# Down-projections with two slices of the second panel first, norm rows by a repeated column, a last norm on three engines, and a new order of some copies and low parts

## What is computed

```python
def first_block(x, ...):
    u = rmsnorm(h, norm1_g)
    proj = u @ w_in            # GDN q,k,v,z; DSA q,k,v; indexer; branch gates
    o_gdn = rmsnorm(gated_delta_rule(conv, silu, l2norm of q,k,v ...)) * silu(z)   # 8 heads of 128
    o_dsa = dsa_sparse_attention(...)      # 8 heads, the best 128 keys of an indexer
    h = h + (sigmoid(gate_a) * o_gdn + sigmoid(gate_b) * o_dsa) @ w_out
    up = causal_dwconv(rmsnorm(h, norm2_g) @ ffn_w_up) + ffn_conv_b
    h = h + (silu(up_gate) * up_value) @ ffn_w_down          # inner width 2816
    return rmsnorm(h, final_g)

def second_block(x, ...):
    # layer 0: FOX attention (16 heads of 64, with a decay bias), SwiGLU
    # layer 1: MLA attention (16 heads, 64 + 32 rotary), SwiGLU
    return rmsnorm(h, final_norm)
```

## Time and profile before

| | us |
|---|---|
| median of 3 runs (lowest, highest) | 2257.74 (2256.88, 2258.3) |
| the profiled execution's own time | 2261.33 |
| its span, first to last instruction | 2259.0 |
| busy: PE / DVE / ACT / POOL | 2203.9 / 1285.7 / 917.2 / 479.6 |
| mean granted clock of TensorE | 0.994 of full |

### The profile page before, as it was taken

One profiled execution on the slowest core, in us unless ns is written; L12 is line 12 of the kernel. 1 busy time (PEld: TensorE's weight loads), 2 busy tenths in 40 slices (PEclk: granted clock), 3 DMA queues, 4 the chain that ended last, 5 costly groups with the idle time before them and its releaser, 6 DMA issues.

```text
span 2259.0 us, 27466 instructions
## 1 busy us (share of the span) xinstructions
PE 2203.9 (98%) x10368; PEld 1805.7 (80%) x10368; DVE 1285.7 (57%) x2142; ACT 917.2 (41%) x1629; POOL 479.6 (21%) x358
## 2 busy tenths in 40 slices
PE   6999999999999999999999999999999999999997
PEld 4887888888887888788887888888777778888885
DVE  7668434677486584846775434334666664434333
ACT  5677433435422222245774322222445553223222
POOL 0000431242311010153672110101232321101012
PEclk9999999999999999999999999999999999999998
DMA  4231311232323323222112332332321123333332
GB/s 161 91 113 57 94 57 47 67 101 63 98 84 103 92 95 93 88 92 91 57 57 66 91 101 94 101 95 87 92 86 57 47 64 93 94 102 94 94 97 80
DMA packets 69011, 193.93 MB, mean 86 GB/s; under 512 B 14608, under 2 KB 18960, under 8 KB 68880
## 3 DMA queue, kind: packets, MB, share of 16 engines
q1 hardware_dynamic: 67584, 189.82, 27.2%
q10 hardware_dynamic: 1296, 2.36, 0.4%
HBM read 185.34 MB, written 6.82 MB: 85 GB/s over the span
## 4 chain that ended last, share of the span: by engine, by line
PE 85%; DVE 5%; issue 4%; ACT 3%; POOL 2%; DMA 1%; POOLq 0%; DVEq 0%; SPq 0%; ACTq 0%
PE bank L306 17%; PE bank L308 17%; PE bank L307 17%; PE bank L342 7%; PE bank L344 7%; PE bank L343 7%; PE bank L1658 2%; PE bank L991 1%; PE bank L1370 1%; PE bank L1684 1%; PE bank L1685 1%; ACT b_wh L247 1%; PE bank L1034 1%; PE bank L1906 1%; ACT b_arena L1738 1%
## 5 line engine op out<-in xcount | busy, mean ns | idle before, releaser
L247 ACT ACTIVATE b_wh<-b_raw 128x1024 fp32r<-128x1024 f32 (+1 forms) x348 | 358.4, 1030 | 1077.0 <-PE bank L308 841.8
L306 PE MATMUL bank<-b_xh,b_wh 128*128 128x512 f32 x1080 | 422.6, 391 | 0.4 <-DVE b_wl L252 0.3
L308 PE MATMUL bank<-b_xh,b_wl 128*128 128x512 f32 x1080 | 420.5, 389 | 0.0
L307 PE MATMUL bank<-b_xl,b_wh 128*128 128x512 f32 x1080 | 420.3, 389 | 0.0
L252 DVE TENSOR_TENSOR b_wl<-b_raw,b_wh 128x1024 fp32r<-128x1024 f32 (+1 forms) x298 | 362.7, 1217 | 98.2 <-ACT b_wh L247 97.7
L342 PE MATMUL bank<-b_xh,b_wh 128*128 128x512 f32 x760 | 317.2, 417 | 5.0 <-DVE b_xl L2160 3.8
L344 PE MATMUL bank<-b_xh,b_wl 128*128 128x512 f32 x760 | 298.6, 393 | 0.0
L598 POOL TENSOR_TENSOR b_yl<-b_arena,b_yh 128x512 fp32r<-128x512 f32 x66 | 112.0, 1697 | 877.4 <-ACT b_yh L576 877.4
L343 PE MATMUL bank<-b_xl,b_wh 128*128 128x512 f32 x760 | 297.6, 392 | 0.0
L306 PE MATMUL bank<-b_yh,b_wh 128*128 128x512 f32 x720 | 283.3, 393 | 7.4 <-POOL b_yl L598 7.0
L308 PE MATMUL bank<-b_yh,b_wl 128*128 128x512 f32 x720 | 281.0, 390 | 0.0
(11 more groups left out here) (394 smaller groups left out, 3064.6 us busy)
## 6 DMA issues: line engine op xcount, KB each, us to landing
b_raw<-in_zga SPq DMA_DIRECT2D x16, 512.0 KB, 3.6
b_raw<-in_c0up SPq DMA_DIRECT2D x16, 512.0 KB, 3.5
b_raw<-in_c1up SPq DMA_DIRECT2D x16, 512.0 KB, 3.5
b_raw<-in_fqk SPq DMA_DIRECT2D x16, 512.0 KB, 3.5
b_raw<-in_s0up SPq DMA_DIRECT2D x16, 512.0 KB, 3.6
b_raw<-in_s1up SPq DMA_DIRECT2D x16, 512.0 KB, 3.5
b_raw<-in_m0up SPq DMA_DIRECT2D x16, 512.0 KB, 3.5
b_raw<-in_m1up SPq DMA_DIRECT2D x16, 512.0 KB, 3.5
```

What stands on the lines that cost most here:

```text
L247: act.activation(wh[:, par, cols], raw[:, par, cols], ACT.Copy).then_inc(w_hi, 1)
L306: pe.matmul(bank[:, :], wh[:, par, w], hi[:, x, :], start=(k == 0), stop=False)
L307: pe.matmul(bank[:, :], wh[:, par, w], lo[:, x, :], start=False, stop=False)
L308: last = pe.matmul(bank[:, :], wl[:, par, w], hi[:, x, :], start=False, stop=(k == kt - 1))
```

## The change

It has these parts:

- The down-projections of c, s and m are issued by `products_down`: slices 0 to k-2 of panel 0, slices 0 and 1 of panel 1, the last slice of panel 0, the rest of panel 1, then the other panels.
- The norm's row is `row_of`: four matmuls, each with one column of `rowT` repeated 128 times as the stationary operand and the identity as the moving one, in place of ones by the diagonal. DVE's diagonal and its wait for POOL's power go (`late_diag` becomes `late_mean`). Only `final1` and the row behind it keep the diagonal.
- The last norm: POOL sums seven squares, PE sums the eighth from ACT's tile directly into another bank, DVE adds the two. ACT multiplies the tiles by the gain ahead of the row (`gained`); DVE multiplies six by the row, POOL two, and the output goes in the order 0, 1, 2, 3, 6, 4, 5, 7.
- Delta rule: ACT's split and gate go from the end of level 0 to level 1, the split behind the copies of L1076, the gate behind those of L1081.
- FOX: the split of panel `fqk+2` goes ahead of the first head's projection on ACT and DVE. `low(2)` stands ahead of `scaled` from head 13 on, and in MLA in head 14 too. POOL's `yl` goes from the start of odd heads to the end of the even heads before them; MLA's stays in its head but behind the (in MLA absent) projection.

```diff
@@ -287,6 +287,16 @@
+        def products_down(pe, seg, ready):
+
+            kt, base = KT[seg], BASE[seg]
+            for t, k in [(0, k) for k in range(kt - 1)] + [(1, 0), (1, 1), (0, kt - 1)] + [(1, k) for k in range(2, kt)]:
+                n = base + t
+                if t == 0:
+                    pe.wait_ge(*ready(k))
+                slice_k(pe, n, n % 2, k, kt, yh, yl, 0, base if t == 1 else None)
+            products(pe, seg, yh, yl, first=2)
+
         def products(pe, seg, hi, lo, tile0=0, ready=None, between=None, first=0):
@@ -369,6 +379,12 @@
+        def row_of(pe, bank):
+
+            for b in range(NB):
+                m = pe.matmul(bank[:, B(b)], rowT[:, b:b + 1].broadcast_to([P, P]), ident, start=True, stop=True)
+            return m
+
         def norm_pe(pe, name, src=None, weights=None, row=True):
@@ -381,21 +397,12 @@
         def norm_pe_row(pe, name):
-            pe.wait_ge(n_dg, NROW[name] + 1)
-            pe.matmul(pb[6][:, :], ones, diag[:, :], start=True, stop=True).then_inc(n_row, 1)
-
-        def norm_pool(pool, name):
-            cnt, dst, own = NORMS[name]
-            if own:
-                pool.wait_ge(n_ev, NROW[name] + 1)
-                pool.tensor_tensor(rowT[:, :], rowT[:, :], mhalf[:, 0:NB], ALU.pow).then_inc(n_pw, 1)
-            if dst != "h":
-                hi, lo, rdy = (xh, xl, x_ready) if dst == "x" else (yh, yl, y_ready)
-                t0 = 2 if name == "cqn" else 0
-                for t in range(cnt):
-                    pool.wait_ge(n_hi, NHI[name] + t + 1)
-                    pool.tensor_tensor(lo[:, t0 + t, :], tmpb[:, t % 2, :], hi[:, t0 + t, :].bitcast(F32),
-                                       ALU.subtract).then_inc(rdy, 1)
+            if name == "final1":
+                pe.wait_ge(n_dg, 1)
+                pe.matmul(pb[6][:, :], ones, diag[:, :], start=True, stop=True).then_inc(n_row, 1)
+                return
+            pe.wait_ge(n_pw, NROW[name] + 1)
+            row_of(pe, pb[6]).then_inc(n_row, 1)
@@ -403,8 +410,6 @@
                 dve.tensor_scalar(rowT[:, :], pb[7][:, 0:NB], 1.0 / dim, EPS, ALU.mult, ALU.add).then_inc(n_ev, 1)
-                dve.wait_ge(n_pw, n)
-                dve.tensor_tensor(blk(diag[:, :]), rep(ident, NB), bc(rowT[:, :], P), ALU.mult).then_inc(n_dg, 1)
                 if between is not None:
@@ -454,12 +459,10 @@
-        def late_diag(dve, name, dim):
+        def late_mean(dve, name, dim):
             n = NROW[name] + 1
 ...
             dve.tensor_scalar(rowT[:, :], pb[7][:, 0:NB], 1.0 / dim, EPS, ALU.mult, ALU.add).then_inc(n_ev, 1)
-            dve.wait_ge(n_pw, n)
-            dve.tensor_tensor(blk(diag[:, :]), rep(ident, NB), bc(rowT[:, :], P), ALU.mult).then_inc(n_dg, 1)
@@ -521,6 +524,7 @@
         sg, cg, cv, pr = (take(j * T, T) for j in range(4))
+        gained = take(8 * T, 8, T)
         raws = [take((4 + j) * T, T) for j in range(2)]
@@ -1074,13 +1078,16 @@
                         act.activation(t0_[s], gbanks(s)[0][:, :], ACT.Copy).then_inc(g_t0s, 1)
+                    if lv == 1 and three:
+                        n = PAIR0[i]
+                        split_hi(act, n + 2, n // 2 + 1, n % 2, 8)
                     for s in range(2):
 ...
                         act.activation(yy[s], gbanks(s)[2][:, :], ACT.Copy).then_inc(g_ys, 1)
-                    if lv == 0 and three:
-                        gate(PAIR0[i])
+                    if lv == 1 and three:
+                        gate_act(act, PAIR0[i])
                 for s in range(2):
@@ -1836,7 +1843,7 @@
                     project_dve(dve, h_ + 2)
-                low_first = A.name == "mla" and h_ != 14
+                low_first = A.name == "mla" or h_ >= 13
                 if 0 <= h_ < 16:
@@ -1880,16 +1887,17 @@
                     split_lo(pool, n, n // 2, n % 2, KT_OF[n])
-                if h_ >= 3 and h_ % 2 == 1:
-                    t = (h_ - 3) // 2
-                    if h_ == 15:
-                        pool.wait_ge(h_n, A.first + 16)
-                    pool.wait_ge(yh_done, YH[{"fox": "foxo", "mla": "mlao"}[A.name]] + t + 1)
-                    pool.tensor_tensor(yl[:, t, :], A.y[t % 2], yh[:, t, :].bitcast(F32), ALU.subtract).then_inc(h_f, 1)
                 if A.name == "fox" and 0 <= h_ and h_ + 2 < 16:
 ...
                     one_hot(pool, h_ + 3)
+                lag = 0 if A.name == "fox" else 1
+                if h_ - lag in range(2, 15, 2):
+                    t = (h_ - lag) // 2 - 1
+                    if t == 6:
+                        pool.wait_ge(h_n, A.first + 16)
+                    pool.wait_ge(yh_done, YH[{"fox": "foxo", "mla": "mlao"}[A.name]] + t + 1)
+                    pool.tensor_tensor(yl[:, t, :], A.y[t % 2], yh[:, t, :].bitcast(F32), ALU.subtract).then_inc(h_f, 1)
@@ -1919,7 +1927,7 @@
             if A.name == "fox":
-                act.wait_ge(n_dg, NROW["final1"] + 1)
+                act.wait_ge(n_dg, 1)
             for b in range(NB):
@@ -1987,8 +1995,11 @@
                 (conv_load if seg in ("misc", "gk", "gq", "gv", "zga") else load)(sp, seg)
-            for t in range(DT):
-                sp.wait_ge(n_tmp, NTMP["final2"] + t + 1)
+            for t in (0, 1, 2, 3, 6, 4, 5, 7):
+                if t < 6:
+                    sp.wait_ge(n_tmp, NTMP["final2"] + t + 1)
+                else:
+                    sp.wait_ge(n_pw, NROW["final2"] + 1 + t - 5)
                 sp.dma_start(out[t], h[:, t, :]).then_inc(s_out, 16)
@@ -2046,8 +2057,12 @@
                 hidden_pool(pool, "m", ch)
-            sum_squares(pool, "m2dn", 8)
-            norm_pool(pool, "final2")
+            sum_squares(pool, "m2dn", 7)
+            late_pool(pool, "final2")
+            pool.wait_ge(n_dg, 3)
+            for t in (6, 7):
+                pool.wait_ge(n_hi, NHI["final2"] + t + 1)
+                pool.tensor_tensor(h[:, t, :], gained[:, t, :], rrow[:, :], ALU.mult).then_inc(n_pw, 1)
@@ -2085,9 +2100,9 @@
             split_and(act, split_hi, "fv1", fv1_act)
+            split_hi(act, BASE["fqk"] + 2, BASE["fqk"] // 2 + 1, BASE["fqk"] % 2, 8)
             act.wait_ge(f_3, 1)
             project_act(act, 0)
-            split_hi(act, BASE["fqk"] + 2, BASE["fqk"] // 2 + 1, BASE["fqk"] % 2, 8)
             heads_act(act, FOX)
@@ -2132,9 +2147,14 @@
             split_and(act, split_hi, "mo", square_h(act, "mo", "fn1"))
+
+            def m2dn_act(n, t, q, r, bank):
+                act.wait_ge(out_free, n + 1)
+                square(act, "m2dn", t, r, h[:, t, :])
+                act.activation(gained[:, t, :], h[:, t, :], ACT.Copy, scale=V("final2", t)).then_inc(n_hi, 1)
             for ch in range(3):
                 hidden_act(act, "m", ch)
-                split_and(act, split_hi, f"m{ch}dn", square_h(act, "m2dn") if ch == 2 else None)
+                split_and(act, split_hi, f"m{ch}dn", m2dn_act if ch == 2 else None)
@@ -2146,7 +2166,7 @@
             dve.wait_ge(s_const, 32)
-            late_diag(dve, "norm1", D)
+            late_mean(dve, "norm1", D)
             split_lo(dve, 0, 0, 0, KT_OF[0])
@@ -2167,7 +2187,7 @@
             split_and(dve, split_lo, "wout", add_to_h(dve, "norm2", None, True), True)
-            late_diag(dve, "norm2", D)
+            late_mean(dve, "norm2", D)
@@ -2221,18 +2241,18 @@
             project(dve, FOX, 0)
+            split_lo(dve, BASE["fqk"] + 2, BASE["fqk"] // 2 + 1, BASE["fqk"] % 2, 8)
             project_dve(dve, 0)
-            split_lo(dve, BASE["fqk"] + 2, BASE["fqk"] // 2 + 1, BASE["fqk"] % 2, 8)
             project(dve, FOX, 1)
 ...
             split_and(dve, split_lo, "fo", add_to_h(dve, "fn0"), True)
-            late_diag(dve, "fn0", D)
+            late_mean(dve, "fn0", D)
             for ch in range(3):
 ...
                     rope_dve(dve)
-            late_diag(dve, "kvn", D)
+            late_mean(dve, "kvn", D)
@@ -2253,7 +2273,7 @@
                 if t == 2:
-                    late_diag(dve, "ckvn", 256)
+                    late_mean(dve, "ckvn", 256)
                 if t == 3:
@@ -2277,7 +2297,7 @@
                 if t == 0:
-                    late_diag(dve, "cqn", 768)
+                    late_mean(dve, "cqn", 768)
             split_and(dve, split_lo, "uk", uk_post)
@@ -2290,11 +2310,21 @@
             split_and(dve, split_lo, "mo", add_to_h(dve, "fn1"), True)
-            late_diag(dve, "fn1", D)
+            late_mean(dve, "fn1", D)
             for ch in range(3):
 ...
                 split_and(dve, split_lo, f"m{ch}dn", add_to_h(dve), True)
-            norm_dve(dve, "final2", h, D, "final2")
+            dve.wait_ge(n_ms, NROW["final2"] + 1)
+            dve.tensor_scalar(rowT[:, :], pb[7][:, 0:NB], 1.0 / D, EPS, ALU.mult, ALU.add)
+            dve.drain()
+            dve.wait_ge(n_ms, NROW["final2"] + 2)
+            dve.scalar_tensor_tensor(out=rowT[:, :], in0=pb[4][:, 0:NB], scalar=1.0 / D, in1=rowT[:, :],
```

(25 more changed lines are left out.)

## The result

The changed kernel took 2244.77 us (median of 4 runs, 2244.31 to 2245.39), the kernel before beside it 2257.65. The ratio is 0.9943, with a 95% interval of 0.9926 to 0.996: 12.9 us or 0.57% less. Forecast were 21.8 us less, with a range down to 13.7 less. The sign was right, and the size and the range were not. The two profiled executions differ by more, since the one of the kernel before lay 3.6 us above its median: the span was 2259.0 and is 2242.6, 16.4 less.

What follows compares the result with a forecast made beforehand. TensorE, busy 98% of the span, was taken as the bound, so only its small waits and the tail could pay. Terms 8.2+1.5+3.8+1.9+1.0+1.0+3.8+0.6 = 21.8 us off the 2257.7 median gave 2236, range 2230.5 to 2244.

Steps and rivals of the forecast that it cites:

- The turns: Up- into down-projections of c, s, m: reordered down panels shorten PE's waits for low parts, 8.2 us saved.
- The 1.6 for c2's slow slices: After c2's turn: a shorter wait lets slices run at full pace instead of 1.28 us each, 1.6 us saved.
- The norm rows: Norms: DVE's diagonal goes and the row is made from a repeated column in eight records, 1.5 us saved.
- The tail: After the last product: POOL's last addition and the diagonal go, multiplications are shared with POOL, 3.8 us saved.
- The delta rule: Delta rule: ACT's split and gate no longer stand ahead of copies PE waits for, 1.9 us saved.
- The FOX start: Start of FOX: the split moves away from POOL's cast, removing PE's wait, 1.0 us saved.
- The FOX heads: FOX heads: moving `yl` gains 2.1 us in odd heads, less 1.1 for one even-head collision, 1.0 us saved.
- rival 1: FOX heads: port collision in all seven even heads, their term -5.6 instead of 1.0, giving 2242.6 us; chance 0.18.
- The last heads: Last FOX heads: third low part ahead of DVE's scaling saves 3.8 us, 1.5 of it clock; MLA 0.6.
- Rival 2: Norm rows: the repeated column loads slowly, their term -5 instead of 1.5, giving 2242.5 us; chance 0.10.
- rival 3: Down-projection turns: waits move to panel 1's low weights and the slow clock stays, about 4 us less gain, 2240; chance 0.10.
- Rival 4: FOX even heads: collisions are followed by a clock fall, 4.1 us in each of seven heads, giving 2263.5 us; chance 0.03.

Runs made afterwards that it cites:

- `only_down`: The kernel before with the new order of the down panels alone: 2251.73 us, ratio 0.9968.
- `rows_old`: The changed kernel with all norm rows but the last by the diagonal again: 2246.59 us, ratio 0.9944.
- `tail_old`: The changed kernel with the last norm as before, but its row still by a repeated column: 2246.17 us, ratio 0.9947.
- `again`: The kernel before, unedited, profiled once more: median 2259.59 us over ten executions, ratio 1.0001.
- `gdn_old`: The changed kernel with ACT's split and gate at the end of the delta rule's level 0 again: 2246.93 us, ratio 0.9949.
- `yl_back`: The changed kernel with POOL's `yl` back at the start of odd FOX heads: 2241.83 us, ratio 0.9923.
- `yl_wait`: The changed kernel with `yl` in even FOX heads also waiting until DVE has scaled the next head's probabilities: 2237.97 us, ratio 0.9907.
- `low_old`: The changed kernel with the third low part again behind the scaling at the last FOX heads and MLA head 14: 2248.39 us, ratio 0.995.
- `only_yl`: The kernel before with only POOL's `yl` of the FOX heads moved to even heads: 2261.8 us, ratio 1.0016.
- `whole`: The changed kernel, unedited, timed on the same chip as its parts: 2244.72 us, ratio 0.9938.

## Why the forecast missed

- **The turns** (8.2 forecast): 7.3 by `only_down`. The waits went as worked out (c0 0.29 left, c2 1.38, s2 none). The 1.6 for c2's slow slices is the doubtful part. The pace holds behind c2's turn in all ten profiles with the new order, but it also held in one of three with the old one. The lower level near 994 us comes with either order. So the median can pay part of the 1.6 and not the whole, and how large a part was not settled.
- **The norm rows** (1.5): 1.9 by `rows_old`. Eight records took 1.05 where 1.01 was estimated. In the first norm, where the whole 0.69 was to come, none came: from the start of POOL's power to the row it was 1.79 us and is 1.97. DVE's split, freed from its wait for the power, now stretches the power from 1.01 to 1.92. I had put that freed wait at nothing. So the gain lies in the other rows; the traces show some 1.2 of the 1.9, and the medians can't bound it more closely.
- **The tail** (3.8): the two profiles differ by 3.8, but `tail_old` costs 1.45 by medians, and with the diagonal's 0.7 on top it is about 2.2; by the tails of all profiles it is about 3.3 (17.3 less 14.0). The term was read from an execution whose lower level began before the sums had ended: they took 1.82, and 1.05 in `again`.
- **The delta rule** (1.9): 2.2 by `gdn_old`. Right, and the cover for DVE's gate held: the list of waits after names none for the level's subtraction.
- **The FOX start** (1.0): the wait went from 1.0 to 0.6. POOL's cast takes 0.87 rather than 1.41, but DVE's subtraction ahead (L1723) takes 1.79 rather than 0.68, beside a POOL operation.
- **The FOX heads** (1.0): this is the step that failed. The forecast was one head with a collision and 2.1 gained in odd heads. (The 2.1 is itself a slip: six heads by 0.4 are 2.4.) There were six with a collision, at 1.07 each, and five odd heads that gained 0.35 each: -4.7, which is most of the way to rival 1 (-5.6, chance 0.18). The sixth odd head is the last interval and belongs to the next point. The failing sentence is that `yl` "is ready just as DVE's fourth scaling begins" since ACT's high part ends at 1109.52. That end was read off a head whose timing was itself set by `yl` in the odd head ahead of it. `yl_back` and `yl_wait` show both phases, 0.60 and 0.17 behind the scaling's start. The one head of the earlier trace rows ahead of which no `yl` stands, at 1089.92, had the right phase. I treated it as the exception, and it was the rule: POOL free at 1090.88, 0.96 after the scaling's start, and `yl` 0.16 later, 1.12, as measured. The section on the shared port in the Trainium skill ("SBUF — State Buffer", "SBUF: two separate sides") says that the first to start holds the pair for the whole instruction. The trace agrees that one is held up for the whole length of the other: DVE's third scaling, not the fourth, lasts until `yl` ends, 1.39 instead of 0.27. Who came first the records do not show: the third scaling begins 0.02 ahead of `yl`, and `yl` 0.06 before the end of the second.
- **The last heads** (3.8 and 0.6): `low_old` costs 3.7 over both, of which the traces show 1.2 in FOX and 0.7 in MLA. The wait of 1.73 went with the move of `yl` (the last interval falls from 9.36 to 7.99 in `only_yl`), 1.4 us. The 1.5 for the clock is not paid by every execution: `again` has the same waits of 1.74 and 0.94 with the clock at 1.00, while `only_down`, with waits of 1.74 and 1.11, has the lower level again.

Worked together by the medians: turns 7.3, rows 1.9, tail 1.45 and its diagonal 0.7, delta rule 2.2, `yl` -2.9, low parts 3.7, and by the trace 0.5 at the FOX start, is 14.9, against 14.6 for `whole`. With terms that are each uncertain by 1 us or more, that this comes out so closely is luck. Against the 21.8 forecast, the heads and the last heads together gave 0.8 rather than 5.4, which is 4.6 of the 6.9; the tail lacks 1.65, the turns 0.9, the FOX start 0.5, and rows and delta rule gave 0.7 more. The sign came right since the other parts outweigh the one that lost. The range ended at 2244.0, because rival 1 was taken alone, and never together with clock terms that the median pays only in part: the profiled execution stood 3.6 us over the median, and I subtracted savings read from it, its lower clock included, from the median. Some of it the median does pay. Of the 39 executions of the kernel before, 7 had a mean clock of 0.997 and took 2255.8 to 2257.2, and the others less clock and more time; the nine of the changed kernel all had 0.997 or 0.998. At 0.997 the change is thus worth 11 to 12 us, and the rest of the 14.6 came with a higher mean clock, to which the shorter tail, at the lower level in every profile, belongs. Rival 2 is refuted. Of rival 3 the small waits of c0 to c2 are true, but the slow clock behind c2 did not stay. Rival 4 did not come: waits of 0.86 in six heads brought no lower level.

## What to carry to other kernels

An operation moved to a gap must be laid beside the timing that the gap will have once it is moved, and a head that is free of it already shows that timing. Where two engines hold each other up, a short wait on the idle one, here 0.75 us on POOL, is cheaper than luck in the order. Taking a wait off an engine can start such a collision elsewhere, as the first norm's power shows. Savings at the lower clock level are to be counted in full only if more than one profile shows the same stretch at that level; here a profile above its median had more of it than the median pays.

## What was not expected of the hardware

POOL's power of 128x4 elements, 1.01 us by itself, took 1.92 beside a split on DVE of 1.21 us that began 0.16 before it (in `yl_wait`), so an operation with next to no data was held up by 0.9. And one kernel's executions differ by 6 us with the mean granted clock (0.997 to 0.994). The stretches at the lower level come and go at the same few places, behind waits of PE that other profiles show without them: behind c2's turn (a wait of 2.5), near 994 us (0.5) and at the last FOX heads (1.7). In `yl_wait` one stands in the delta rule.
